# Modulation of a two-layer block: product and sums of every tile in one VectorE operation, twelve of 48 tiles early

## What is computed

```
def modulate(h, shift, scale):
    return h * (1.0 + scale) + shift

def adaln_params(cond, w, b):
    mod = jax.nn.silu(cond) @ w + b
    return jnp.split(mod[..., None, :], 6, axis=-1)
```

## Time and profile before

| | |
|---|---|
| median of 3 runs | 1061.9 us (1061.57 to 1061.93) |
| the profiled execution's own time | 1061.37 us |
| its span | 1059.3 us |
| PE busy | 1040.0 us (98%) |
| DVE, ACT, POOL busy | 665.7, 418.6, 543.7 us |
| moved by DMA | 131.92 MB, mean 125 GB/s |

### The profile page before, as it was taken

The page is one execution under the profiler, slowest core; times in us unless marked ns, Lnnn a source line. Parts: engine busy times, 40 slices in busy tenths (PEclk is TensorE's granted clock), DMA queues, the critical chain, the costliest instruction groups (busy, mean ns, idle before and its releaser), DMA issues.

```text
span 1059.3 us, 13471 instructions
## 1 busy us (share of the span) xinstructions
PE 1040.0 (98%) x4968; PEld 856.4 (81%) x4968; DVE 665.7 (63%) x1007; ACT 418.6 (40%) x687; POOL 543.7 (51%) x401
## 2 busy tenths in 40 slices
PE   7999999999999999999999999999999999999996
PEld 5889887877877888778888888778888888888885
DVE  5663776866499765985788847386666666520503
ACT  6223547665554243644444342442323223221222
POOL 1688895999200064234444346535465545553641
PEclk9999999999999999999999999999999999999999
DMA  6446454342446922212322113303222232223222
GB/s 257 164 168 225 133 187 153 90 163 70 179 159 238 379 104 100 93 67 80 110 83 84 54 42 155 143 33 146 87 80 79 103 135 79 80 80 135 104 80 79
DMA packets 19611, 131.92 MB, mean 125 GB/s; under 512 B 3411, under 2 KB 3811, under 8 KB 13030
## 3 DMA queue, kind: packets, MB, share of 16 engines
q1 hardware_dynamic: 8784, 92.62, 23.2%
q0 software_dynamic: 6560, 27.27, 8.0%
q10 hardware_dynamic: 4214, 11.30, 2.8%
HBM read 124.90 MB, written 6.30 MB: 124 GB/s over the span
## 4 chain that ended last, share of the span: by engine, by line
PE 95%; DVE 2%; ACT 1%; DMA 1%; issue 0%; POOL 0%; SPq 0%; POOLq 0%; ACTq 0%; DVEq 0%
PE bank L505 81%; PE bank L496 7%; PE bank L511 3%; PE bank L752 1%; PE bank L746 1%; DMA x_sb<-x_in 1%; PE bank L904 1%; PE bank L741 1%; DVE arena L2178 0%; DVE arena L2181 0%; PE bank L913 0%; PE bank L753 0%; PE bank L869 0%; ACT arena L1189 0%; DVE arena L2214 0%
## 5 line engine op out<-in xcount | busy, mean ns | idle before, releaser
L1730 POOL TENSOR_TENSOR ring_parts<-ring,ring_parts 128x1024 fp32r<-128x1024 f32 x102 | 248.7, 2442 | 266.3 <-ACT ring_parts L1189 263.5
L505 PE MATMUL bank<-hT_parts,ring_parts 128*128 128x512 f32 x1344 | 339.2, 393 | 0.8 <-ACT hT_parts L1518 0.8
L1189 ACT ACTIVATE ring_parts<-ring 128x1024 fp32r<-128x1024 f32 (+2 forms) x163 | 168.6, 1043 | 383.7 <-PE bank L505 219.9
L505 PEld LDWEIGHTS bank<-hT_parts,ring_parts 128*128 128x128 f32 x1344 | 249.6, 188 | 54.7 <-ACT hT_parts L1518 2.4
L505 PE MATMUL bank<-ring_parts,hT_parts 128*128 128x512 f32 (+1 forms) x672 | 171.6, 379 | 1.0 <-POOL ring_parts L1730 0.6
L505 PE MATMUL bank<-ring_parts,arena_parts 128*128 128x512 f32 (+1 forms) x736 | 172.4, 386 | 0.0
L505 PEld LDWEIGHTS bank<-ring_parts,arena_parts 128*128 128x128 f32 x736 | 136.6, 188 | 27.9 <-DVE arena L2416 0.3
L505 PE MATMUL bank<-arena_parts,ring_parts 128*128 128x512 f32 x592 | 148.0, 391 | 0.3 <-DVE arena_parts L2285 0.3
L505 PEld LDWEIGHTS bank<-ring_parts,hT_parts 128*128 128x128 f32 x672 | 122.4, 188 | 22.8 <-POOL ring_parts L1730 1.0
L2521 DVE SCALAR_TENSOR_TENSOR arena<-bank,small,arena 128x441 f32<-128x441 f32 (+2 forms) x176 | 122.3, 695 | 24.6 <-DVE arena L2521 1.7
L505 PEld LDWEIGHTS bank<-arena_parts,ring_parts 128*128 128x128 f32 x592 | 111.0, 188 | 25.4 <-DVE arena_parts L2285 2.1
(11 more groups left out here) (223 smaller groups left out, 1100.5 us busy)
## 6 DMA issues: line engine op xcount, KB each, us to landing
ring<-weights_in SPq DMA_DIRECT2D x39, 2048.0 KB, 8.0
arena<-mod_w_in POOLq DMA_DIRECT2D x32, 512.0 KB, 4.1
arena<-mod_w_in POOLq DMA_DIRECT2D x8, 1024.0 KB, 5.5
x_sb<-x_in SPq DMA_DIRECT2D x4, 512.0 KB, 5.7
ring<-weights_in SPq DMA_DIRECT2D x4, 512.0 KB, 8.5
mod_spill<-mod_part POOLq DMA_DIRECT2D x16, 128.0 KB, 2.1
x_sb<-x_in ACTq DMA_DIRECT2D x4, 512.0 KB, 12.2
arena<-mod_spill ACTq DMA_DIRECT2D x1, 2048.0 KB, 10.6
```

Of the source, the lines that this page charges most:

```text
L505: ins = nc.tensor.matmul(out, l, r, start=start and n == 0, stop=stop and n == len(passes) - 1)
L1189: return nc.scalar.activation(out, in_, ACT.Copy)
L1730: return nc.gpsimd.tensor_tensor(part(low), low, part(high), ALU.subtract)
```

## The change

All 48 tiles of the modulation (128 columns each, laid out with a column of the matrix per partition, so 128 x 1024) go to DVE. `cond` is broadcast to all partitions (512 KB, into the first half of `mod_g`) and put through Silu there by ACT, as one operation of 128 x 1024 behind piece 8. For each tile DVE issues one `scalar_tensor_tensor` with an accumulator: tile times `cond_row`, summed over the free dimension into one column of `modc`. Tiles 0 to 11 run in the projection stage in four buffers, tiles 12 to 39 two behind each of the fourteen pieces of the gate stage, 40 to 47 among the merge tiles, again in four buffers. The bias is added on DVE before the output tiles. The two gates go out of `modc` to a DRAM row as single numbers (128 x 16 elements) and come back by one broadcast load into `mod_g`. POOL only issues the loads; its products and additions, the spill, the load back, the matmuls at L904 and L913 and the copies behind them are gone. In DVE's list `scale_n2(3)` now stands ahead of `add_abs(6)`. `mod_part` becomes `minus` (same size) and `modc` moves behind the large buffer `arena`, padding keeps the address of `arena`: 115328 bytes in both programs.

```diff
-MOD_AFTER = (9, 11, 13, 15, 16, 17, 18, 19)
-ROOTS_AFTER = (11, 21, 23, 25, 27)
-PAUSE_AFTER = 17
+MOD_TILES = 6 * KD
+MOD_EARLY = 12
...
-        modw_dve = [at(65, 2048, KD), at(75, 2048, KD)]
-        modw_pool = [at(99, 1024, KD), at(103, 1024, KD)]
+        cond_row = mod_g[:, 0, :]
+        modw_early = [at(99, D), at(103, D), at(65, D), mod_g[:, 1, :]]
+        modw_late = [at(75, D), at(79, D), at(65, D), at(69, D)]
...
-            modulation(0)
-            gate_rows(0)
             wo_tile(0)
             wo_tile(1)
-            modulation(1)
-            gate_rows(1)
             filter_tile(0)
             wo_tile(2)
-            modulation(2)
...
             wo_tile(7)
-            gate_rows(2)
-            gate_rows(3)
-            modulation(3)
...
             for p in range(4, 15):
                 split_high(p)
+                if p == 8:
+                    wait("cond_in", 16)
+                    nc.scalar.activation(cond_row, cond_row, ACT.Silu).then_inc(sem("cond_ready"), 1)
...
-            wait("mod_dve_done", MOD_DVE)
-            act.dma_start(mod_back, mod_spill_d).then_inc(sem("mod_back_in"), 16)
...
             for p in range(FIRST_PD + 5, FIRST_PD + 8):
                 split_high(p)
+            wait("mod_summed", MOD_TILES)
+            act.dma_start(at(75, 1024), tables_d[:, 0:1024]).then_inc(sem("tables_in"), 16)
...
             square_x2(TT - 1)
 
+            wait("gates_ready", 1)
+            act.dma_start(mod_row_d.rearrange("a (t p) -> p (a t)", p=P), modc[:, 4 * KD:MOD_TILES],
+                          allow_slow_non_contiguous=True).then_inc(sem("mod_row_out"), 16)
...
+            def load_mod(j):
+                if j < MOD_EARLY:
+                    b, buffers, name = j % len(modw_early), modw_early, "modw_early"
+                    used = j - len(modw_early) + 1
                 else:
+                    b, buffers, name = (j - MOD_EARLY) % len(modw_late), modw_late, "modw_late"
+                    used = j - len(modw_late) + 1 if j >= MOD_EARLY + len(modw_late) else 0
+                if used > 0:
+                    wait("mod_summed", used)
+                pool.dma_start(buffers[b], mod_d[:, j * D:(j + 1) * D]).then_inc(sem(f"{name}{b}"), 16)
...
+            chunk_landed(pool, C_DK)
+            pool.dma_start(cond_row, cond_d.partition_broadcast(P).rearrange("p a d -> p (a d)")).then_inc(sem("cond_in"), 16)
+            for j in range(MOD_EARLY):
+                load_mod(j)
+                if j == 11:
                     latent_roots()
+            for h in range(HEADS):
+                head_roots(h)
+            wait("o_ready", HEADS)
+            load_mod(MOD_EARLY)
+            load_mod(MOD_EARLY + 1)
+            wait("pv_done", 4 * UNITS)
+            for j in range(MOD_EARLY + 2, MOD_TILES):
+                load_mod(j)
...
+            def mod_tile(j):
...
+                V.scalar_tensor_tensor(out=w, in0=w, scalar=1.0, in1=cond_row, op0=ALU.mult, op1=ALU.mult,
+                                       accum_out=modc[:, j:j + 1]).then_inc(sem("mod_summed"), 1)
...
             for p in range(FIRST_GATE + 6, FIRST_PD + 4):
                 split_low(p)
+                for j in range(2):
+                    mod_tile(MOD_EARLY + 2 * (p - FIRST_GATE - 6) + j)
...
+                if d == 1:
+                    for j in range(MOD_TILES - 8, MOD_TILES - 4):
+                        mod_tile(j)
                 if d % 2:
                     split_low(FIRST_PD + 4 + d // 2)
+                    mod_tile(MOD_TILES - 4 + d // 2)
...
             norm_x2(2)
-            modg_late(2)
             norm_x2(3)
-            modulation()
             scale_n2(2)
-            modg_late(3)
+            scale_n2(3)
             add_abs(6)
-            scale_n2(3)
```

More of the change, by code:

```diff
@@ L392, in build_program @@
         NORM_BANK = (2, 1)
-        MODG_BANK = (2, 2, 4, 5)
         N2_BANKS = (1, 2)
@@ L1224, in _ @@
                     split_high(2 + k // 2)
-            nc.scalar.activation(st(CSILU, KD), small[:, SMALL["cond"]], ACT.Silu).then_inc(sem("cond_ready"), 1)
             for i, t in enumerate((sin_t, cos_t)):
@@ L2107, in split_output, with modulation @@
                 V.tensor_tensor(part(low), low, part(high), ALU.subtract).then_inc(sem("oT_low"), 1)
+            def modulation():
+                wait("mod_summed", MOD_TILES)
+                V.tensor_tensor(modc[:], modc[:], small[:, SMALL["mod_b"]], ALU.add).then_inc(sem("gates_ready"), 1)
+                wait("gates_ready", 1)
+                for s, name in enumerate(("norm_g1", "norm_g2")):
+                    c = modc[:, (2 * s + 1) * KD:(2 * s + 2) * KD]
+                    ins = V.scalar_tensor_tensor(out=c, in0=c, scalar=1.0, in1=small[:, SMALL[name]], op0=ALU.add, op1=ALU.mult)
+                ins.then_inc(sem("modc_ready"), 1)
             wait("lambda_exps", 1)
@@ L2160, in _ @@
             split_low(FIRST_WO + 3)
[L2163 to L2170 removed]
+            modulation()
             def add_abs(i):
```

155 lines of the change are left out of this document (31 added, 124 removed).

## The result

The changed kernel is slower, by 0.24%: 1064.96 us, median of 11 runs (1062.52 to 1067.06), against 1061.93 us for the kernel before in the same session (11 runs, 1061.57 to 1062.57). The ratio is 1.0024, 95% interval 1.0015 to 1.0034. The forecast was 1057.2 us with a range up to 1061.5. What is new is also the scatter: 4.5 us between executions, where the kernel before has 1.0.

What follows compares the result with a forecast made beforehand. PE, busy 98% of the span, was taken as the bound. Terms -1.0 - 4.33 + 0.3 + 0.4 = -4.6 us took 1061.37 to 1056.8, stated as 1057.2 us because median neighbours lie 0.5 higher; range 1053.5 to 1061.5.

Steps and rivals of the forecast that it cites:

- Between the output tiles, 4.33 us: Between output tiles: removing PE's modulation matmuls and a gate row piece there gains the full 4.33 us.
- Ahead of the first output tile, -1.0 us: Output tile 0 starts sooner, but waits for the last merged copy and DVE's subtractions: gain 1.0 us, not 2.65.
- The tile, 1.3 us: One DVE modulation tile of 128 x 1024 with accumulator takes 1.3 us, upper bound 1.9 us.
- rival A: DVE's accumulating form is slow, 2.4 us a tile, so PE waits 27 us from the gate stage on: 1084 us; 7%.
- Eight tiles among the merge tiles: zero: Merge stage: eight tiles add 10.4 us to DVE, pieces stay ahead of PE, DVE catches up: zero cost.
- Rival C: Loads late, hitting merge pieces from 11 us on, or the first network layer late: 1059 to 1064 us; 14%.
- Behind the last output tile, +0.3 us: Behind the last output tile, removed matmuls buy about 0.2 us and DVE's new order costs 0.5: net loss 0.3 us.
- Rival D: PE's granted clock falls behind the new 2.2 us idle stretch after the last output tile: up to 8.7 us, 1061; 5%.
- The gate stage, +0.4: Gate stage with 28 tiles: the first network layer's margin is 0.1 to 0.2 us; 0.4 us lost, 0 to 1.5.
- DVE's three terms for this stage: Gate stage DVE work: 14 pieces of 1.13 us, 28 tiles at 36.4 us, three network layers of 4.7 us; about 69 us.

Runs made afterwards that it cites:

- experiment 3: Changed kernel with add_abs(6) back ahead of scale_n2(3) on DVE and x reloaded only behind all 48 sums: 1057.39 us.
- experiment 9: The kernel of experiment 3 with ACT's two decay exponentials moved ahead of its copy of the last merged tile: 1058.84 us, repeated at 1057.75 us.
- experiment 5: Changed kernel, its DVE order kept, with x reloaded behind all 48 sums and POOL waiting for add_abs(6) before its four subtractions: 1057.36 us.
- experiment 6: Kernel before with only scale_n2(3) moved ahead of add_abs(6) in DVE's list: 1065.34 us.
- experiment 4: Kernel before with PE's modulation matmuls and gate rows cut to stubs: 1061.33 us; also without the second gate row and with ACT's copies cut: 1058.70 us.
- h2_mid_x_late: Changed kernel with add_abs(6) ahead of scale_n2(3), eight tiles moved from merge stage to attention units, x reloaded behind the last sum: 1055.68 us, repeated at 1055.63.

## Why the prediction was wrong

Point by point, by its own steps.

- *Between the output tiles, 4.33 us*: right, 4.53 measured.
- *Ahead of the first output tile, -1.0 us*: the mechanism was right, and the size where nothing else is late (-0.69 in experiment 3). In the changed kernel the place cost +3.38, for a reason that the step did not look at.
- *The tile, 1.3 us, and rival A*: right. 1.22 us, 1.15 from one to the next, no wait for it. The page of the Trainium skill that was weighed here ("Vector Engine (DVE) Microarchitecture Reference", "Points that are easy to get wrong": half throughput with two SBUF sources that are not bf16, no port for the accumulator) does not hold for this form as the prediction read it, a tile at twice a plain operation: 1.22 us is no more than the form without accumulator and than a plain subtraction of this size (L1828, 1.22).
- *Eight tiles among the merge tiles: zero*: **this step failed.** It laid out DVE's own durations and took every load as there; the landing time that the layout went by, 4.1 us, is a median over the whole kernel before. Landing took 9.6 us, five tiles waited 8.3 us together, and DVE's last merge, whose slack was never counted, came 3.3 us late. (Up to 4.9 us of such waits were made up for, in experiment 9.) Rival C named late loads, but from 11 us on and for the merge pieces; what went late was DVE's own merge list behind the tiles. It had 14%, and its price of 1059 to 1064 did not have the second loss in it.
- *Behind the last output tile, +0.3 us*: **this step failed too.** It priced the new order at 0.5 us, with `add_abs(6)` at 1.4 us; the operation took 3.4. The rows had shown what POOL's subtraction does to DVE (3.45 us for two pieces against 3.50 for three), `add_abs` itself stood at 2.94 and 2.75 us in the trace before, and the step did not ask what POOL would start once `scale_n2(3)` came sooner. With POOL held back (experiment 5) T to D grows by 0.46 us over before, where the step said 0.3; with POOL beside it, by 5.01. Alone the swap costs 3.3 us (experiment 6).
- *Rival D, the clock*: it was costed as a case of its own, for the idle time behind T. There it does happen, in six of twelve profiled executions, and costs 0.9 to 1.4 us where it does, not 4. But it also follows each of the two waits above. In output tile 0 the place cost 4.07 us over experiment 3: 3.04 because DVE was late, and 1.03 for the clock, counted from 393.41, since up to there DVE would have held PE in any case. Behind T it cost 5.20: 0.65 for the order, 2.05 for the longer wait beside POOL, 2.50 for the clock. Of the 9.3 us at the two places 3.5 are clock. The rule of the Trainium skill ("TensorE: Matmul & The Clock Gate", "HAM oscillation"), that PE idle between bursts falls back to the lower level, agrees with the falls here, which follow idle stretches of 1.9 to 3.2 us, though not in every execution.
- *The gate stage, +0.4*: M came 0.67 us later, but PE had no wait there. The delay was already there at 114 us, most of it (0.63) from a stretch whose pace varies in both kernels (see below). The term was nearer to 0. (DVE's three terms for this stage add up to 66 us, not 69; nothing hangs on it.)

With both failed steps undone the kernel ran at 1057.39 us, where the forecast said 1057.2. That they agree to 0.2 us is in part luck. The profiled execution took 1055.55 us where the terms give 1056.8: the forecast has 0.5 us for an order that is undone here, and nothing for the 0.65 us of the last stores. The median stands higher, as far as is known for the falls of the clock behind T, which the forecast left out.

## What to carry to other kernels

A wait of some 2 us put on PE where it was dense until then can cost more than its length: in these traces the lower clock behind it took 0.9 to 2.5 us more. It does not come every time (six of twelve where the wait was 2 us), so expect scatter. When a step is moved ahead in one engine's list, ask what the other engines start from it, and whether that runs into the list's next instruction. And price a load by the busiest stretch that it falls into, not by a median over the whole kernel, and count the slack of the list behind the instruction that waits for it.

## What was unexpected of the hardware

- One `TENSOR_TENSOR` of 128x512 on DVE, all operands in SBUF: 0.69 us alone, 2.75 us beside POOL's subtractions of 128x1024 (10.15 us for four). That is four times, where the pieces had shown one and a half. The operation ahead of it, of the same size, took 0.69: it had started at 452.24, before POOL's at 452.40. The ones behind it with an operand in a bank took 0.69 beside POOL too (L2238 at 456.35, L2246 at 457.14). It looks less like slower work than like a wait for the subtraction that POOL has under way: taken one by one, POOL's first of the four runs from 452.40 to 455.15, and DVE's operation ends at 455.70; the two of the kernel before at 417.77 and 420.75 also end some 0.55 us behind one of POOL's. No run here tests it.
- The same wait of 2.60 us, in the same kernel and place, left the clock full in one execution and at its lower level for some 3 us in another (0.89 on average over 385 to 400 us).
- PE's stretch of 192 narrow matmuls at 82 to 114 us took 31.04 us in the changed kernel and 30.41 before, with no wait. Both paces occur in both kinds: in the stubbed kernel before of experiment 4 the slow one, in experiments 3 and 8 (h2_mid_x_late) the fast one. What makes it is open; it is 0.6 us.
